# A table for the turns of the weight splits in a state-space scan, with the second gate and the output's steps one turn earlier

## The reference

```python
# 32 heads of 64 columns, 8 groups, chunked scan
xbc = silu(conv(xbc));  xs, Bm, Cm = split(xbc)
Lmat = exp(seg)                                      # decay between tokens, per head
CB = einsum('bclgn,bcsgn->bcgls', Cc, Bc)            # per group of four heads
y_diag = einsum('bcgls,bcgrls,bcsgrp->bclgrp', CB, Lmat, X)
...
y = rmsnorm(y * silu(z), ssd_norm)
y_b = y @ w_o_ssd                                    # the output
mix = (sigmoid(g_a) * y_a + sigmoid(g_b) * y_b) @ w_out   # g_b = h @ w_in[:, gate b]
```

## Time and profile before

| | us |
|---|---|
| median of 3 runs | 972.31 (971.44 to 973.08) |
| profiled execution | 969.64 |
| its span | 967.9 |
| TensorE busy | 941.1 (97%) |
| VectorE busy | 663.4 (69%) |
| ScalarE busy | 539.5 (56%) |
| GpSimd busy | 235.7 (24%) |
| share of TensorE in the chain that ended last | 84% |

### The profile page before, as it was taken

The page is one execution under the profiler, slowest core; times in us unless marked ns, Lnnn a source line. Parts: engine busy times, 40 slices in busy tenths (PEclk is TensorE's granted clock), DMA queues, the critical chain, the costliest instruction groups (busy, mean ns, idle before and its releaser), DMA issues.

```text
span 967.9 us, 15371 instructions
## 1 busy us (share of the span) xinstructions
PE 941.1 (97%) x5665; PEld 801.0 (83%) x5665; DVE 663.4 (69%) x1094; ACT 539.5 (56%) x952; POOL 235.7 (24%) x235
## 2 busy tenths in 40 slices
PE   8999999999999999999999999999999999999997
PEld 8987778888877898999878899976678878888786
DVE  5765677777785668965578666677866767755453
ACT  6667575444534668744455466566764654544443
POOL 5304102111122240399932144320200021000100
PEclk9999999999999999999999999999999999999999
DMA  9755357799887813750139666642254777656562
GB/s 287 237 149 178 107 153 256 231 282 279 279 279 238 254 45 118 209 153 22 46 124 340 189 182 188 171 136 66 87 179 149 252 236 236 209 178 193 194 216 69
DMA packets 131352, 179.00 MB, mean 185 GB/s; under 512 B 8124, under 2 KB 96910, under 8 KB 131280
## 3 DMA queue, kind: packets, MB, share of 16 engines
q1 hardware_dynamic: 120384, 144.53, 47.8%
q0 software_dynamic: 10304, 33.18, 11.3%
q10 hardware_dynamic: 592, 0.34, 0.1%
HBM read 176.90 MB, written 1.12 MB: 184 GB/s over the span
## 4 chain that ended last, share of the span: by engine, by line
PE 84%; DVE 7%; ACT 4%; DMA 2%; issue 2%; DVEq 0%; SPq 0%; ACTq 0%
PE bank L1942 17%; PE bank L2022 16%; PE bank L2024 16%; PE bank L2023 16%; DVE w_lo L1333 2%; PE bank L2195 1%; PE bank L2458 1%; DMA w_raw<-in_w_in 1%; PE bank L1973 1%; PE bank L2454 1%; PE bank L2481 1%; DMA w_raw<-in_w_down 1%; ACT w_hi L868 1%; PE bank L2389 1%; PE bank L2077 1%
## 5 line engine op out<-in xcount | busy, mean ns | idle before, releaser
L1333 DVE TENSOR_TENSOR w_lo<-w_raw,w_hi 128x1024 fp32r<-128x1024 f32 (+1 forms) x239 | 282.7, 1206 | 86.9 <-ACT w_hi L868 86.4
L868 ACT ACTIVATE w_hi<-w_raw 128x1024 fp32r<-128x1024 f32 (+1 forms) x266 | 270.4, 1038 | 117.0 <-PE bank L2024 71.1
L2022 PE MATMUL bank<-w_hi,h_hi 128*128 128x512 f32 x448 | 179.2, 400 | 3.4 <-DVE w_lo L1333 3.4
L2024 PE MATMUL bank<-w_hi,h_lo 128*128 128x512 f32 x448 | 174.8, 390 | 0.0
L2023 PE MATMUL bank<-w_lo,h_hi 128*128 128x512 f32 x448 | 174.4, 389 | 0.0
L1942 PE MATMUL bank<-h_hi,w_hi 128*128 128x256 f32 x432 | 124.4, 288 | 2.1 <-DVE h_lo L1486 1.1
L1942 PE MATMUL bank<-h_lo,w_hi 128*128 128x256 f32 x432 | 122.1, 283 | 0.0
L1942 PE MATMUL bank<-h_hi,w_lo 128*128 128x256 f32 x432 | 122.1, 283 | 0.0
L2022 PE MATMUL bank<-w_hi,ff_hi 128*128 128x512 f32 x272 | 107.8, 396 | 3.4 <-DVE w_lo L1333 2.2
L2023 PE MATMUL bank<-w_lo,ff_hi 128*128 128x512 f32 x272 | 106.0, 390 | 0.0
L2024 PE MATMUL bank<-w_hi,ff_lo 128*128 128x512 f32 x272 | 105.9, 389 | 0.0
(11 more groups left out here) (461 smaller groups left out, 1595.9 us busy)
## 6 DMA issues: line engine op xcount, KB each, us to landing
w_raw<-in_w_in SPq DMA_DIRECT2D x84, 512.0 KB, 3.8
ada_raw<-in_ada_w POOLq DMA_DIRECT2D x48, 512.0 KB, 6.3
w_raw<-in_w_gate_up SPq DMA_DIRECT2D x88, 256.0 KB, 5.3
w_raw<-in_w_ffn_in SPq DMA_DIRECT2D x88, 256.0 KB, 4.0
w_raw<-in_w_down SPq DMA_DIRECT2D x22, 512.0 KB, 6.5
w_raw<-in_w_ffn_out SPq DMA_DIRECT2D x22, 512.0 KB, 4.6
w_raw<-in_w_out SPq DMA_DIRECT2D x16, 512.0 KB, 3.6
w_raw<-in_w_o_ssd SPq DMA_DIRECT2D x16, 512.0 KB, 3.6
```

The source lines that it names most:

```text
L868: act.activation(high(u, n), w_raw[:, u % RING, 0:n], ACT.Copy).then_inc(hi_ready, 1)
L1333: return dve.tensor_tensor(dst, src, hi.bitcast(F32), ALU.subtract)
L2022: pe.matmul(out, x_hi[:, k, x], hi, start=start, stop=False, skip_group_check=True)
L2024: return pe.matmul(out, x_lo[:, k, x], hi, start=False, stop=stop, skip_group_check=True)
```

## The change

The turns of the splits now come from a table. `SCAN_UNITS[i]` is the number of units that are split by the end of turn i; turns that it does not name split nothing. Unit 2 moves ahead of the scan: on ScalarE before the silu of the last convolution block, on VectorE before the last times-dt product. `GB_STEPS` puts four steps instead of three behind heads 0 and 1, none behind head 10 (before: 12), and ends at head 26 (before: 28). `GB_READ` moves both copies one turn earlier. `OS_STEPS` gives turn 14 two output steps.

```diff
-    GB_STEPS = [3 if h < 2 else 0 if h == 12 or h > 28 else 1 for h in range(2 * KI)]
-    GB_READ = (5, 14)
-    OS_STEPS = {KI - 1: 2, KI: 4, KI + 1: 4}
+    GB_STEPS = [4 if h < 2 else 0 if h == 10 or h > 26 else 1 for h in range(2 * KI)]
+    GB_READ = (4, 13)
+    OS_STEPS = {KI - 2: 2, KI - 1: 2, KI: 4, KI + 1: 4}
+    SCAN_UNITS = {0: 4, 3: 5, 4: 6, 7: 7, 8: 8, 10: 9, 11: 10, 13: 11, 14: 12, 17: 13, 18: 14}
...
@@ ScalarE, convolution @@
+            if b == s_xbc.n:
+                split_to(s_gb.u0 + 3)
             if b >= 1:
                 act.wait_ge(dve_read, s_xbc.dve0 + b)
...
@@ ScalarE, scan @@
-            if i % 2 == 0:
-                split_to(s_gb.u0 + i // 2 + 1 + AHEAD)
+            if i in SCAN_UNITS:
+                split_to(s_gb.u0 + SCAN_UNITS[i])
...
```

## The result

The changed kernel took 964.26 us, median of 4 runs (963.95 to 966.32), against 972.12 for the kernel before in the same comparison (4 runs, 971.44 to 973.08). The ratio is 0.9923, 95% interval 0.9906 to 0.994. It is faster, by 7.9 us, where 5.15 had been forecast from 972.31.

The account below looks back on a forecast made before the run. TensorE was taken to bound the kernel. Its waits removed, 6.27 us, less waits added, 1.12, gave a net 5.15, so 972.31 - 5.15 = 967.2 us (chance 0.60), range 965.2 to 970.2.

Parts of the forecast that it names:

- four waits for `w_lo`: TensorE's waits in the scan for VectorE's splits of weight units; all go, gaining 2.01, 1.88 and 0.76 us.
- the one at head 2: TensorE's wait for ScalarE's first exponential before head 2's pair product; two more steps cover it, gain 0.37 us.
- the two new waits: TensorE waits for ScalarE's gate copies, each behind a split in turns 4 and 13; 0.50 and 0.62 us added.
- The net of the scan: Waits removed, 6.27 us, less waits added, 1.12: a gain of 5.15 us, all on TensorE.
- 6 x 0.16: Added to six bracketed TensorE waits, 5.31 us, because by starts each loses 0.16 more; total 6.3 us.
- the terms of the splits and of the copies: Scan: split waits removed, 2.01, 1.88 and 0.76 us; copy wait of 1.25 removed, 0.50 and 0.62 added.
- A: The new copy waits in the scan don't appear; gain 6.3 us, time 966.0; chance 0.12.
- C: Splits still come behind the same late products, so waits of 1.85 and 0.78 us stay; time 972, chance 0.04.
- D: VectorE becomes the pace from head 8 to 28; net 1 us slower, or 3 slower, 975; chance 0.04.
- B: One or two waits of TensorE elsewhere, tightest at the output's unit 6 (margin 0.9 us), cost 1 to 3; chance 0.20.
- GpSimd's folds: Splits in turns 7 and 10 meet them on VectorE, up to 0.8 us late each; cost 0 to TensorE.
- How the numbers follow: Closing step: the 2.67 us between profiled execution and median is carried over, so 972.31 less 5.15 gives 967.2 us.

Follow-up runs that it names:

- splits_only: The changed kernel with the gate's steps, its copies and the output's steps put back as before; 965.3 us, ratio 0.9944 to the kernel before.
- copy_turns_free: The changed kernel with unit 5's split moved from turn 4 to 5 and the output's unit 2's from 13 to 12; 963.0 us, ratio 0.9919.
- copy_first: The changed kernel with ScalarE's copy of the gate's sums ahead of the split in turns 4 and 13; 964.77 us, ratio 0.994.
- before_again: The kernel before, unedited, run again; 970.89 us, ratio 0.9999.
- late_copy_3: The changed kernel with two more ScalarE copies of the gate's first half ahead of the real ones; 967.32 us, ratio 0.9957.
- unit3_alone: The kernel before with unit 2 split ahead of the scan and unit 3 in turn 0, all else as before; 967.78 us, ratio 0.9967.
- after_again: The changed kernel, unedited, run again; 965.25 us, ratio 0.9941 to the kernel before.
- copy_turns_free_tail: As copy_turns_free, with ScalarE also splitting the output's unit 6 between the two pairs of sigmoids; 963.43 us, ratio 0.9921.
- all_but_unit3: The changed kernel with units 2 and 3 split where they were before, and steps and copies as before; 968.0 us, ratio 0.9972.

## Why the prediction was wrong

**What held.** All four waits for `w_lo` went, and so did the one at head 2. The forecast of the two new waits, 0.50 and 0.62 near 660.5 and 691, stands against 0.49 and 0.58 at 660.6 and 691.1. Head 28 was forecast near 689 and starts at 689.07, the output's step near 704 and starts at 704.09; head 0's product at 645.8 stands at 645.77. The net of the scan was forecast at 5.15 and measured at 5.5. The remaining 0.35 is less than the 6 x 0.16 added for six waits, so that term may hold it; no run separates it. `splits_only` and `copy_turns_free` bear out the terms of the splits and of the copies. Rivals A, C and D did not happen. B's tightest place, the output's unit 6, held in the changed kernel; it broke by 0.15 us in `copy_first`, where 0.3 of the scan was won. Two splits met GpSimd's folds and took up to 0.7 us longer, but that costs nothing in front of TensorE, as forecast: no wait of TensorE in the scan names a split.

**The step that failed** is the one in "How the numbers follow": "The median of the runs, 972.31, lies 2.67 above the profiled one, so I carry the difference over". It took the 2.67 for something outside the change and gave it no term and no reason. About half of it, 1.4, was the clock behind the very wait that the change removes: from the profiled 969.64 it is 0.3 to the median of the later runs with a mean clock of 1.000 (969.92), 1.4 from there to the median of all later runs on that chip (971.32), and 1.0 from there to the 972.31 of the first three runs. The profiled execution of before was one without the drop, and the waits are the same with the drop and without, so nothing in its rows priced it. Where the drop comes it costs 1.5 to 1.6 us (`before_again` against before, `late_copy_3`). How often it comes in before can be read only roughly from the mean granted clock of each run, since a fall of the clock at the end of the program lowers that mean too (the profile of `splits_only` has 0.998 and no drop in its scan, but a clock of 0.50 from 960 us to its end at 963.4). Of 55 runs of before and `before_again`, 15 had a mean clock of 1.000 (969.16 to 970.94, median 969.84) and 32 had 0.998 or less (970.68 to 972.78, median 971.4). Without the wait the mean clock does not sort the times: in `splits_only` the two runs at 0.998 took 965.15 and 965.3 and the two at 1.000 took 965.0 and 965.73.

**The sum with that term.** On one chip the five runs of before with a clock of 1.000 had a median of 969.92 and all fifteen 971.32, so the drop lifts the median by about 1.4, as far as the mean clock tells the two kinds apart. The changed kernel stood at 965.25. 969.92 - 965.25 = 4.7 is the part by waits (forecast 5.15, by the two profiles of the scan 5.5), 1.4 the part by clock, together the 6.1 measured there. `unit3_alone` shows the second part by itself: 2.0 by waits, 3.2 measured; and against the three runs of before on that chip with a clock of 1.000 (median 969.67) it gained 1.9, the wait alone.

**What stays open.** The comparison that was to be predicted shows 7.9, not 6.1. The rest, 1.8, is not explained by the change: its four runs of before lie 0.8 above the fifteen later ones, its four of after 1.0 below the five. Other stages differ by such amounts from one execution to the next. By the starts of the same matmuls, `after_again` lost 1.2 us against after between 746 and 781 us, and against before `copy_first` lost 1.4 and `copy_turns_free_tail` 2.2 between 163 and 342 us, where no edit lies. The 0.9 us by which the range was missed is of that size; with the clock's term the forecast would have been 965.8, inside the range but still 1.5 above the median of those four runs. So part of the miss is explained and part stays open.

## What to carry to other kernels

A wait on a busy TensorE can cost more than its idle time: here waits of 1.59, 1.85 and 2.85 us in the scan brought 3.4 us at half clock with them in many executions and not in all, so a profile can show the wait and not its whole price. Before the difference between a profiled execution and the median is carried over, ask what in the changed stretch could vary from run to run, and look at the spread and the clocks of all runs, not at one trace. Do not place a split of a unit beside a copy for which TensorE is about to wait, in the same turn of the same engine; moving two splits to other turns gave the last 0.9 us of the scan.

## What the runs showed of the hardware

The clock drop was not expected. With idle brackets of 1.85 us (`before_again`), 1.59 (`late_copy_3`) and 2.85 (`late_copy_5`) the granted clock went to 0.50 for 3.4 us, nearly all of it while TensorE was busy again; behind the same bracket of 1.85 us it stayed at 1.00 in before and in `all_but_unit3`, and so it did behind one of 1.77 us in another stage of `copy_turns_free_tail`. Behind brackets of 0.2 to 1.1 us in the scan no profile here shows it. What decides between the two is not shown by any run. The 128x512 matmul takes 0.63 us at the lower level and 0.39 at the upper. The cost, 1.4 to 1.6 us, did not grow with the wait.
